# Tokens loaded already turned, with the row factor applied at two evictions and by scaling in place

## The chip, the cores and the metric

One core of one Trainium2 chip runs one launch. Five engines work side by side: TensorE (PE, matmul), VectorE (DVE), ScalarE (ACT), GpSimd (POOL) and SyncE (SP), which issues nearly all transfers. They meet only through semaphores. The metric is the device time of one execution in microseconds (us).

## The reference, cut to what matters

```python
h = x * rsqrt(mean(x*x, -1) + 1e-6) * norm1_w        # x: 512 tokens x 1024
y = h @ w_in                                          # 1024 x 3852, float32
# y is split into the columns of three head groups (forgetting attention,
# retention, gated delta rule) and of their gates:
log_f = log_sigmoid(ff + fox_forget_bias)
log_a = -exp(a_log) * softplus(ga + dt_bias); beta = sigmoid(gb)
qkv = silu(causal_depthwise_conv(concat(gq, gk, gv), conv_w))
x = x + concat(o_fox, o_ret, o_gdn) @ w_out
x = x + hier_moe(rms_norm(x))                         # top-1 group, top-2 of 8 experts
out = rms_norm(x, final_norm_w)
```

The row factor `rsqrt(...)` is one number for each token, `norm1_w` one number for each of the 1024 features. Both can be applied before the product; the row factor can as well be applied to the rows of `y` after it.

## The kernel before, in words

A float32 product is made of three products of reduced operands: each operand is split into a high part (an fp32r copy) and a low part (the operand less its high part), and PE adds high x high, high x low and low x high in one bank of PSUM (`granule`, L750).

**Granules.** The input projection has 15 column groups (`GROUPS`), each of 256 or 260 columns, and each group two granules: the rows of `w_in` in chunks 0 to 3 (even granule) and 4 to 7 (odd). Groups of kind "n" give tokens on partitions (four tiles of tokens, 12 matmuls each and granule, the tokens as the stationary operand), those of kind "t" give columns on partitions (two blocks of 12 matmuls over all 512 tokens). Groups 0 (`zb`, with the gate columns of the delta rule) and 1 (`fv`, with the forget gate) are of kind "n", groups 2 to 7 (`v0` to `q1`) of kind "t".

**The weights' path.** For granule g: SP loads `raw` (L585, three buffers, so from g = 3 on it waits until the low part of g - 3 is made), ACT copies it into `whi` (`weight_high`, L1201, two buffers: it waits until PE has used granule g - 2), POOL subtracts into `wlo` (`weight_low`, L1509), and PE waits for `wlo_done`. POOL does this for every granule; DVE has no part in it.

**The tokens' path.** SP loads four tiles of `x` (L574, tokens on partitions). ACT sums the squares of a tile (`squares`, L1224), DVE takes the reciprocal and multiplies the tile by row factor and by `norm1_w` (`normalize`, L1679), the latter spread over partitions in PSUM by a one-row product (L874). PE turns the tile (`turn_tokens`, L879, eight transposes a tile, those of tiles 2 and 3 between the tiles of granule 0), ACT copies the turned tile into `hHi` (`high_part`, L1229), DVE subtracts into `hLo` (`token_low`, L1693). Granule 0 goes tile by tile behind this.

**What hangs on the first groups.** ACT evicts a group of kind "n" tile by tile (`evac`, L1250). After group 1, DVE computes the gates (`gates`, L1730), a chain of small dependent operations on SBUF with three exponentials of ACT in it, and PE's next task behind granule 5 (`gcum`, L805) waits for its end (`gates_done`). Each engine runs its own list in program order; `AFTER[g]` holds the tasks that follow granule g on every engine. The convolutions of groups 2 to 7 start with four scaled accumulations (ACT L1289, DVE L1723).

The later stages (the triangular solves, attention and retention, the output projection, the routing and the expert loop, whose weights SP loads as buffers come free) are not touched.

Of the kernel before, what the change touches and what calls it, by code (L numbers as in the profile page):

```python
# [23 lines left out]
F32 = mybir.dt.float32  # L24
# [8 lines left out]
P = 128  # L33
# [19 lines left out]
HB = P // 2  # L53

# [31 lines left out]
for _i in range(NIN):  # L86
    AFTER[2 * _i + 1].append(("evac", _i))
AFTER[3].append(("gates",))
# [35 lines left out]
def tensor_orders():  # L124

    a, b = [("par",), ("nb", 0), ("nb", 1)], [("xT", t, i) for t in range(T) for i in range(2)]
    for g in range(GR_IN):
# [3 lines left out]
        for task in AFTER[g]:  # L131
            if task[0] == "vt":
# [126 lines left out]
def build(nc, consts, x, n1w, w_in, foxb, convw, alog, dtb, gnw, w_out, n2w, rgw, rgb, rew, reb,  # L259
# [13 lines left out]
    with ExitStack() as ctx:  # L273
# [31 lines left out]
        PCW = at("PCW", [P, 4, 12], q0 + 288)  # L305
        PGN = at("PGN", [P, P], q0 + 480)
        assert q0 + 480 + 512 <= C0

        hHi = at("hHi", [P, KC, S], R1, F32R)
# [86 lines left out]
        onesr = small[0:1, 640:768]  # L396
# [6 lines left out]
        s_const = sem("s_const"); s_const2 = sem("s_const2"); s_n1 = sem("s_n1"); s_cw = sem("s_cw"); s_par = sem("s_par")  # L403
        s_x = [sem(f"s_x{t}") for t in range(T)]
        raw_full = [sem(f"raw_full{i}") for i in range(3)]
        whi_done = sem("whi_done"); wlo_done = sem("wlo_done"); half_used = sem("half_used")
        ssx_done = sem("ssx_done"); xn_done = sem("xn_done"); hhi_done = sem("hhi_done")
# [121 lines left out]
        rf_done = sem("rf_done"); one_set = sem("one_set"); pass_done = sem("pass_done"); rw_ready = sem("rw_ready"); lg_used = sem("lg_used"); ssp_done = sem("ssp_done"); ssp_sum = sem("ssp_sum"); r2_done = sem("r2_done")  # L529
# [42 lines left out]
        def _(sp):  # L572
            def tokens(t):
                sp.dma_start(X0[:, t, :], x[0, t * P:(t + 1) * P, :]).then_inc(s_x[t], 16)  # L574

            tokens(0)
            tokens(1)
            sp.dma_start(CT[:, 0:NSTAY], consts[:, 0:NSTAY]).then_inc(s_const, 16)

# [10 lines left out]
            for t in range(2, T):  # L590
                tokens(t)
            for g in (1, 2):
                granule(g)
            sp.dma_start(CT[:, NSTAY:], consts[:, NSTAY:]).then_inc(s_const2, 16)
            for dst, src in ((PDT[:, :], dtb[0:1, :].broadcast_to([P, 4])),
# [5 lines left out]
                sp.dma_start(dst, src).then_inc(s_par, 16)  # L601
            def rows_out():
# [15 lines left out]
            for g in range(3, GR_IN + 4):  # L618
# [11 lines left out]
                if 4 <= g < 12:  # L630
                    sp.dma_start(yd.ap().rearrange("(a p) d -> a p d", p=P)[g - 4], zt[:, :]).then_inc(s_zero, 16)
# [105 lines left out]
        def _(pe):  # L737
# [12 lines left out]
            def granule(g, ready=None, between=None, tiles=range(T)):  # L750
                pe.wait_ge(wlo_done, g + 1)
                n, at, parts, chunks, _, w, kind = GRANULES[g]
                hi, lo = high_of(g), low_of(g)
                for b in tiles if kind == "n" else range(2):
# [4 lines left out]
                    if g == 0:  # L759
                        wait_read(pe, ("xT", b, 0))  # L760
                        wait_read(pe, ("xT", b, 1))
                    for c, kc in enumerate(chunks):
                        if kind == "n":
                            tk = slice(b * P, (b + 1) * P)
                            o = ps[:, 0:w]
                            terms = ((hHi[:, kc, tk], hi[:, c, :]), (hHi[:, kc, tk], lo[:, c, :]),
                                     (hLo[:, kc, tk], hi[:, c, :]))
# [32 lines left out]
            def task(k):  # L800
                if k[0] == "vt":
# [3 lines left out]
                elif k[0] == "gcum":  # L805
                    pe.wait_ge(gates_done, 1)
                    ps = begin(k)
# [61 lines left out]
            par = begin(("par",))  # L869
            pe.wait_ge(one_set, 1)  # L870
            pe.wait_ge(s_n1, 16)
            for i in range(2):
                name = ("nb", i)
                end(pe.matmul(begin(name)[:, :], onesr, n1r[:, i * 512:(i + 1) * 512], start=True, stop=True), name)  # L874
            pe.wait_ge(s_const, 16)
            pe.wait_ge(s_cw, 16)
            end(pe.transpose(par[:, 0:48], PW48[:, :], ident[0:48, 0:48]), ("par",))

            def turn_tokens(t):  # L879
                for i in range(2):  # L880
                    pe.wait_ge(xn_done, 2 * t + i + 1)
                    four(("xT", t, i), lambda c, o: pe.transpose(o, X0[:, t, (4 * i + c) * P:(4 * i + c + 1) * P], ident))

            turn_tokens(0)
            turn_tokens(1)
            for g in range(GR_IN):
                granule(g, between=lambda b: turn_tokens(b + 2) if g == 0 and b + 2 < T else None)
                for k in AFTER[g]:
                    task(k)
# [322 lines left out]
        def _(act):  # L1212
# [7 lines left out]
            act.dma_start(n1r[:, :], n1w[0:1, :]).then_inc(s_n1, 16)  # L1220
            act.dma_start(PW48[:, :], convw[0].rearrange("k (b p) -> (k b) p", p=P)).then_inc(s_cw, 16)
            act.wait_ge(one_set, 1)
            act.activation(rs[0:1, 0:1], rs[0:1, 0:1], ACT.Sqrt)
            def squares(t):  # L1224
                act.wait_ge(s_x[t], 16)
                link(act.activation(junk[:, :], X0[:, t, :], ACT.Square, accum_out=ssx[:, t:t + 1]))
                act.activation(ssx[:, t:t + 1], ssx[:, t:t + 1], ACT.Sqrt, scale=1.0 / D, bias=epsm[:, :]).then_inc(ssx_done, 1)

            def high_part(t):  # L1229
# [1008 lines left out]
```

## Time and profile before

| what | us |
|---|---|
| median of 3 runs | 617.63 (617.51 to 618.59) |
| profiled execution, its own time | 617.34 |
| its span | 615.2 |
| PE busy | 581.6 (95%) |
| DVE, ACT, POOL busy | 239.4, 199.4, 187.3 |

The span is the time from the first to the last recorded instruction of the profiled execution, whose own time is 2.1 us longer. In the rows below "busy" of PE contains the modelled ends of pipelined matmuls, so the starts of consecutive matmuls are the better measure of its pace. "L774" is a line of the kernel before. Where a row counts several instructions, its second number runs from the start of the first to the end of the last.

### The profile page before, as it was taken

What the parts mean: (1) busy time and instruction counts of PE and PEld (TensorE: products, weight loads), DVE (VectorE), ACT (ScalarE), POOL (GpSimd) and SP (SyncE); (2) the same over time, 40 slices, a digit from 0 to 9 for tenths busy, and PEclk for the clock granted to TensorE, in tenths of its full rate; (3) what the DMA queues carried; (4) which work ended last, traced back from release to release, by engine and by line L of the source; (5) the groups of instructions that cost most, each with busy time, mean ns of one, the idle gap of its engine ahead of it and who ended that gap; (6) DMA issues with size and microseconds to landing.
All of it is one profiled execution on the core that took longest, in us unless ns stands there. A gap on an engine that the chain in (4) does not pass through costs nothing.

```text
span 615.2 us, 12002 instructions
## 1 busy us (share of the span) xinstructions
PE 581.6 (95%) x4922; PEld 448.5 (73%) x4922; DVE 239.4 (39%) x588; ACT 199.4 (32%) x437; POOL 187.3 (30%) x128
## 2 busy tenths in 40 slices
PE   7999999999999999999999999999999999997794
PEld 5997887799998888866689998666566565654351
DVE  6225454583116712277542146323332232321117
ACT  6444445433323352544635321111111121110113
POOL 1434344173178423432363301111112111120014
PEclk9999999999999999999999999999999999999998
DMA  9656443421221122002698878999999999999976
GB/s 338 206 158 185 139 122 118 137 70 37 70 70 36 36 70 70 1 2 85 280 357 312 313 269 311 366 412 430 425 422 424 425 428 426 421 428 425 419 317 236
DMA packets 44856, 150.62 MB, mean 245 GB/s; under 512 B 8552, under 2 KB 29760, under 8 KB 38274
## 3 DMA queue, kind: packets, MB, share of 16 engines
q1 hardware_dynamic: 40208, 141.67, 60.6%
q0 software_dynamic: 4528, 8.15, 3.6%
q8 instruction: 40, 0.66, 0.4%
q14 instruction: 14, 0.11, 0.1%
q10 hardware_dynamic: 66, 0.03, 0.0%
HBM read 141.69 MB, written 16.27 MB: 257 GB/s over the span
## 4 chain that ended last, share of the span: by engine, by line
PE 62%; DMA 21%; DVE 8%; issue 4%; ACT 2%; POOL 1%; SPq 0%; DVEq 0%; POOLq 0%; ACTq 0%
PE bank L774 30%; DMA xg<-h2d,tok 13%; PE bank L798 9%; DMA w<-in_expert_w_dram 8%; PE bank L1186 5%; PE bank L1140 3%; PE bank L1162 2%; PE bank L1086 1%; DVE Dm L1823 1%; PE bank L1080 1%; PE bank L1100 1%; PE bank L1056 1%; DMA raw<-in_w_in_dram 1%; PE bank L905 1%; PE bank L972 1%
## 5 line engine op out<-in xcount | busy, mean ns | idle before, releaser
L1511 POOL TENSOR_TENSOR wlo<-raw,whi 128x1024 fp32r<-128x1024 f32 (+1 forms) x25 | 59.9, 2398 | 96.7 <-ACT whi L1209 96.7
L774 PE MATMUL bank<-wlo,hHi 128*128 128x256 f32 (+2 forms) x224 | 65.5, 292 | 0.0
L1140 PE MATMUL bank<-w,xT 128*64 128x256 f32 x512 | 59.6, 386 | 5.7 <-issue 5.7
L1633 POOL DMA_INDIRECT yd<-oy,dst x15 | 15.1, 1009 | 162.3 <-DVE oy L2153 162.3
L774 PE MATMUL bank<-whi,hHi 128*128 128x256 f32 (+1 forms) x208 | 60.6, 291 | 2.8 <-DVE cacc L1723 1.4
L1140 PEld LDWEIGHTS bank<-w,xT 128*64 128x64 f32 x512 | 38.3, 140 | 30.9 <-issue 16.1
L1162 PE MATMUL bank<-w,xT 128*64 128x256 f32 x512 | 58.2, 380 | 2.7 <-DMA w<-in_expert_w_dram 2.7
L1186 PE MATMUL bank<-w,hidT 128*64 128x512 f32 x256 | 58.5, 598 | 1.1 <-ACT hidT L1488 1.1
L774 PE MATMUL bank<-whi,hLo 128*128 128x256 f32 (+1 forms) x208 | 59.2, 285 | 0.0
L1162 PEld LDWEIGHTS bank<-w,xT 128*64 128x64 f32 x512 | 36.5, 137 | 21.6 <-DMA w<-in_expert_w_dram 3.6
L2136 DVE SCALAR_TENSOR_TENSOR hid<-bank,slot,sa 128x256 f32<-128x256 f32 x16 | 10.8, 675 | 96.4 <-issue 93.8
L774 PE MATMUL bank<-hHi,wlo 128*128 128x512 f32 x112 | 44.1, 393 | 0.0
L1209 ACT ACTIVATE whi<-raw 128x1024 fp32r<-128x1024 f32 (+1 forms) x25 | 26.6, 1063 | 51.9 <-PE bank L774 50.3
L774 PEld LDWEIGHTS bank<-wlo,hHi 128*128 128x128 f32 x224 | 42.8, 191 | 0.5
L774 PEld LDWEIGHTS bank<-whi,hHi 128*128 128x128 f32 x208 | 39.7, 191 | 4.2 <-DVE cacc L1723 1.8
L1483 ACT ACTIVATE sa<-bank,slot 128x256 f32<-128x256 f32 x16 | 7.6, 474 | 107.8 <-PE bank L1140 101.4
L774 PEld LDWEIGHTS bank<-whi,hLo 128*128 128x128 f32 x208 | 39.7, 191 | 0.0
L1186 PEld LDWEIGHTS bank<-w,hidT 128*64 128x64 f32 x256 | 17.2, 136 | 29.1 <-issue 27.2
L774 PE MATMUL bank<-hHi,whi 128*128 128x512 f32 x96 | 38.2, 398 | 0.0
L774 PE MATMUL bank<-hLo,whi 128*128 128x512 f32 x96 | 37.8, 394 | 0.0
L774 PE MATMUL bank<-whi_tight,hHi 128*128 128x256 f32 (+1 forms) x112 | 36.9, 330 | 0.5 <-issue 0.4
L1723 DVE SCALAR_TENSOR_TENSOR cacc<-bank,PCW,cacc 128x511 f32<-128x511 f32 (+2 forms) x36 | 26.4, 747 | 23.6 <-ACT cacc L1289 22.4
(375 smaller groups left out, 1124.1 us busy)
## 6 DMA issues: line engine op xcount, KB each, us to landing
w<-in_expert_w_dram SPq DMA_DIRECT2D x44, 2048.0 KB, 21.5
raw<-in_w_in_dram SPq DMA_DIRECT2D x24, 512.0 KB, 3.8
w<-in_expert_w_dram SPq DMA_DIRECT2D x8, 1024.0 KB, 7.1
yd<-zt SPq DMA_DIRECT2D x8, 512.0 KB, 5.1
yt<-yd SPq DMA_DIRECT2D x4, 1024.0 KB, 8.6
raw<-in_w_in_dram SPq DMA_DIRECT2D x6, 520.0 KB, 7.2
X<-in_x_dram SPq DMA_DIRECT2D x4, 512.0 KB, 5.8
raw<-in_w_out_dram SPq DMA_DIRECT2D x4, 512.0 KB, 3.4
```

The costliest lines, as they stand in the source:

```text
L774: m = pe.matmul(o, l, r, start=(at == 0 and c == 0 and i == 0), stop=(at == parts - 1 and kc == chunks[-1] and i == 2), skip_group_check=True)
L798: return pe.matmul(o, l, r, start=True, stop=True)
L905: pe.matmul(two[i][:, 0:w], fqT[hp, pr, t * P:(t + 1) * P], fkT[hp, pr, 0:w], start=True, stop=False)
L1140: m = pe.matmul(pb[3][r, 0:FF], xT[:, c, r], w1[u % 4][:, e, c * FF:(c + 1) * FF], start=(c == 0), stop=(c == KC - 1), skip_group_check=True)
L1162: m = pe.matmul(pb[7][r, 0:FF], xT[:, c, r], w3[u % 4][:, e, c * FF:(c + 1) * FF], start=(c == 0), stop=(c == KC - 1), skip_group_check=True)
L1186: m = pe.matmul(pb[5 + n][r, :], hidT[:, c, r], w2[s][:, e, c * D + n * 512:c * D + (n + 1) * 512], start=(c == 0), stop=(c == 1), skip_gr ...
L1209: e.activation(high_of(g), raw_of(g), ACT.Copy).then_inc(whi_done, 1)
L1483: act.activation(sa[:, :], pb[3][:, 0:FF], ACT.Silu, scale=slot[:, u, 0:1]).then_inc(sa_ready, 1)
L1511: pool.tensor_tensor(low_of(g), raw_of(g), high_of(g).bitcast(F32), ALU.subtract).then_inc(wlo_done, 1)
L1633: pool.indirect_dma_start(yd.ap()[:, :], bass.IndirectOffsetOnAxis(ap=dst_i[o][:, 0:1].bitcast(U32), axis=0), oy[o][:, :], None, bounds_ch ...
L1723: j = dve.scalar_tensor_tensor(out=a[:, s:S], in0=psum(name)[:, 0:S - s], scalar=PCW[:, 3 - s, blk:blk + 1], in1=a[:, s:S], op0=ALU.mult, ...
L2136: dve.scalar_tensor_tensor(out=hid[:, :, :].rearrange("q c p -> q p c"), in0=v(pb[7][:, 0:FF]), scalar=slot[:, u, 1:2], in1=v(sa[:, :]), o ...
```

## The change

Two inputs have another layout: `turned` is `x` with features on partitions (128 partitions x 8 chunks x 512 tokens), `lead` holds `norm1_w` and the convolution weights with features on partitions. The kernel still loads `x` as well, for the sums of squares.

- The product with ones, the transposes of `x` and of the convolution weights, `normalize` and `token_low` go. `hHi0` and `hLo0` are made from `turned` times `norm1_w`, without the row factor, chunk by chunk (ACT, then DVE), and serve granules 0 to 3 (groups 0 and 1).
- Granule 0 is run chunk by chunk over four banks (`first_granule`). Its weights' low part is made half by DVE, half by POOL.
- PE runs 30 bf16 products of zeros ahead of it.
- The copies of groups 0 and 1 out of PSUM multiply by the row factor. ACT therefore waits for it ahead of `evac(0)`.
- A task `rb` on PE behind granule 1 spreads the row factor over the partitions. DVE copies it to `RB`, multiplies the eight chunks of `xt0` by it in place, and makes `hLo` of them; ACT makes `hHi` behind granules 1 and 2. Granules 4 and 5 wait for these.
- The constants' first part is loaded behind granule 3, the second part behind granule 4 and the small parameters.

```diff
+AFTER[1].append(("rb",))
         @block.sync
             granule(0)
-            for t in range(2, T):
-                tokens(t)
-            for g in (1, 2):
-                granule(g)
-            sp.dma_start(CT[:, NSTAY:], consts[:, NSTAY:]).then_inc(s_const2, 16)
+            turned_tokens(0)
+            turned_tokens(1)
+            granule(1)
+            turned_tokens(2)
+            turned_tokens(3)
+            tokens(0)
+            tokens(1)
+            granule(2)
+            tokens(2)
+            tokens(3)
+            sp.wait_ge(first_low, 1)
+            granule(3)
+            sp.dma_start(CT[:, 0:NSTAY], consts[:, 0:NSTAY]).then_inc(s_const, 16)
+            granule(4)
...
         @block.tensor
             def granule(g, ready=None, between=None, tiles=range(T)):
                 pe.wait_ge(wlo_done, g + 1)
+                if g in (1, 4, 5):
+                    pe.wait_ge(xlo_done, {1: KC, 4: KC + HK, 5: 2 * KC}[g])
+                H, L = (hHi0, hLo0) if g < 4 else (hHi, hLo)
...
+            def first_granule():
+                n, _, _, chunks, _, w, _ = GRANULES[0]
+                hi, lo = high_of(0), low_of(0)
+                tiles = [begin(("y", n, b)) for b in range(T)]
+                pe.wait_ge(first_low, 1)
+                for c, kc in enumerate(chunks):
+                    pe.wait_ge(xlo_done, kc + 1)
+                    if c == HK // 2:
+                        pe.wait_ge(wlo_done, 1)
+                    for b in range(T):
...
+                if k[0] == "rb":
+                    pe.wait_ge(s_const, 16)
+                    pe.wait_ge(ssx_done, 2)
+                    four(k, lambda t, o: mm(o, rx[:, t:t + 1].broadcast_to([P, P]), ident))
...
+            zb = zt.bitcast(BF16)
+            pe.wait_ge(zero_set, 1)
+            for _ in range(WARM):
+                pe.matmul(pb[7][:, 0:256], zb[:, 0:P], zb[:, 0:256], start=True, stop=True)
         @block.scalar
+            def high_part(c):
+                act.wait_ge(s_xt[c // 2], 16)
+                act.activation(hHi0[:, c, :], xt0[:, c, :], ACT.Copy, scale=n1p[:, c:c + 1]).then_inc(hhi_done, 1)
+
+            def scaled_high(c):
+                act.wait_ge(tok_scaled, c + 1)
+                act.activation(hHi[:, c, :], xt0[:, c, :], ACT.Copy, scale=n1p[:, c:c + 1]).then_inc(hhi_done, 1)
+
+            weight_high(act, 0)
+            act.wait_ge(s_lead, 16)
+            for c in range(HK):
+                high_part(c)
+            weight_high(act, 1)
+            for c in range(HK, KC):
+                high_part(c)
             squares(0)
             squares(1)
+            weight_high(act, 2)
             squares(2)
             squares(3)
+            act.activation(ssx, ssx, ACT.Sqrt, scale=1.0 / D, bias=epsm[:, :]).then_inc(ssx_done, 1)
+            act.wait_ge(ssx_done, 2)
...
-                        cp = lambda dst, src: act.activation(dst, src, ACT.Copy)
+                        cp = lambda dst, src: act.activation(dst, src, ACT.Copy, scale=rx[:, t:t + 1] if n < 2 else 1.0)
...
+                if g in (1, 2):
+                    for c in range((g - 1) * HK, g * HK):
+                        scaled_high(c)
         @block.vector
+            dve.wait_ge(whi_done, 1)
+            hc = slice(0, HK // 2)
+            dve.tensor_tensor(low_of(0)[:, hc, :], raw_of(0)[:, hc, :], high_of(0)[:, hc, :].bitcast(F32),
+                              ALU.subtract).then_inc(first_low, 1)
+            for c in range(KC):
+                dve.wait_ge(hhi_done, c + 1)
+                dve.scalar_tensor_tensor(out=hLo0[:, c, :], in0=xt0[:, c, :], scalar=n1p[:, c:c + 1],
+                                         in1=hHi0[:, c, :].bitcast(F32), op0=ALU.mult, op1=ALU.subtract).then_inc(xlo_done, 1)
+            dve.wait_ge(ssx_done, 1)
+            dve.reciprocal(rx, ssx).then_inc(ssx_done, 1)
+            name = ("rb",)
+            wait_full(dve, name)
+            release(dve.tensor_copy(RB[:, :], psum(name)[:, :]), name)
+            wait_read(dve, name)
+            dve.wait_ge(xlo_done, KC)
+            for c in range(KC):
+                dve.tensor_tensor(xt0[:, c, :], xt0[:, c, :], RB[:, :], ALU.mult).then_inc(tok_scaled, 1)
+            for c in range(KC):
+                dve.wait_ge(hhi_done, KC + c + 1)
+                dve.scalar_tensor_tensor(out=hLo[:, c, :], in0=xt0[:, c, :], scalar=n1p[:, c:c + 1],
+                                         in1=hHi[:, c, :].bitcast(F32), op0=ALU.mult, op1=ALU.subtract).then_inc(xlo_done, 1)
```

## Rows read from the trace of the kernel before

**Rows 1.** The page, part 1: busy time, share of the span and instructions of each engine.

```profile
PE 581.6 (95%) x4922; PEld 448.5 (73%) x4922; DVE 239.4 (39%) x588; ACT 199.4 (32%) x437; POOL 187.3 (30%) x128
```

**Rows 2.** Chain of waits, 0 to 130 us: start, us, what ran (count).

```profile
20.04 19.05 PE bank L774 x156
50.17 0.04 issue
50.21 0.62 PE bank L798 x4
52.04 11.29 PE bank L774 x48
```

**Rows 3.** Timeline, opening: start, us, engine, line, operation, shapes, count, [idle before, releaser].

```profile
4.53 1.06 ACT L1226 ACTIVATE junk<-X 128x1024 f32<-128x1024 f32 x1 [1.35 <-DMA X<-in_x_dram]
8.26 1.07 ACT L1209 ACTIVATE whi<-raw 128x1040 fp32r<-128x1040 f32 x1 [0.77 <-DMA raw<-in_w_in_dram]
11.87 0.59 PE L774 MATMUL bank<-whi,hHi 128*128 128x260 f32 x1 [1.15 <-POOL wlo L1511]
```

**Rows 4.** Table by window: PE, PEld, DVE, ACT, POOL busy, granted clock, DMA share, GB/s.

```profile
0.00:5.00 5.00, 2.64 (x3) 1.16 (x4) 1.64 (x6) 1.95 (x3) 0.20 (x4) 1.00 0.63 214
5.00:10.00 5.00, 4.41 (x17) 3.14 (x16) 3.19 (x7) 4.17 (x10) 0.59 (x1) 1.00 1.03 387
10.00:15.00 5.00, 3.85 (x18) 3.45 (x17) 4.37 (x9) 3.94 (x9) 1.81 (x1) 1.00 1.09 399
```

**Rows 5.** DVE groups, 0 to 150 us: count, busy us, mean ns, idle before.

```profile
L1686 DVE SCALAR_TENSOR_TENSOR X<-X,keep,bank 128x512 f32<-128x512 f32 x8 | 5.6, 744 | 0.1
L1699 DVE TENSOR_TENSOR hLo<-bank,hHi 128x512 fp32r<-128x512 f32 x8 | 5.1, 684 | 2.0 <-ACT hHi L1233 2.0
```

**Rows 6.** ACT groups, 0 to 150 us.

```profile
L1233 ACT ACTIVATE hHi<-bank 128x512 fp32r<-128x512 f32 x8 | 4.3, 589 | 1.9 <-PE bank L882 1.9
L1209 ACT ACTIVATE whi<-raw 128x1040 fp32r<-128x1040 f32 x4 | 4.3, 1074 | 3.7 <-PE bank L774 2.8 <-DMA raw<-in_w_in_dram 0.8 <-ACT small L1257 0.2
L1226 ACT ACTIVATE junk<-X 128x1024 f32<-128x1024 f32 x4 | 4.2, 1056 | 1.4 <-DMA X<-in_x_dram 1.4
L1257 ACT ACTIVATE fv<-bank 128x256 f32<-128x256 f32 x4 | 1.5, 385 | 3.3 <-PE bank L774 3.3
```

**Rows 7.** Timeline of POOL, 40 to 52 us.

```profile
40.87 2.40 POOL L1511 TENSOR_TENSOR wlo<-raw,whi 128x1024 fp32r<-128x1024 f32 x1 [3.95 <-ACT whi L1209]
45.85 2.40 POOL L1511 TENSOR_TENSOR wlo<-raw,whi 128x1024 fp32r<-128x1024 f32 x1 [2.59 <-ACT whi L1209]
51.71 2.40 POOL L1511 TENSOR_TENSOR wlo<-raw,whi 128x1024 fp32r<-128x1024 f32 x1 [3.45 <-ACT whi L1209]
```

**Rows 8.** Timeline of DVE and ACT, 39 to 51 us: the gates.

```profile
39.63 0.17 DVE L1736 TENSOR_TENSOR small<-small,PDT 128x16 f32<-128x16 f32 x1 [19.74 <-ACTq L1273]
42.10 0.23 ACT L1313 ACTIVATE small<-small 128x32 f32<-128x32 f32 x1
42.56 0.74 DVE L1742 TENSOR_SCALAR small<-small 128x32 f32<-128x32 f32 x1 [2.23 <-ACT small L1315]
45.98 2.33 DVE L1749 SCALAR_TENSOR_TENSOR small<-small 128x32 f32<-128x32 f32 x1
```

**Rows 9.** Timeline of DVE, then of POOL, 307 to 312 us.

```profile
307.34 2.63 DVE L1878 TENSOR_TENSOR mix<-mix,keep 128x1024 f32<-128x1024 f32 x2
...
308.13 0.75 POOL L1602 TENSOR_TENSOR hLo<-foxF,hHi 128x128 fp32r<-128x128 f32 x1 [1.05 <-ACT foxF L1428]
308.85 3.38 POOL L1607 TENSOR_TENSOR mix<-mix,oret 128x1024 f32<-128x1024 f32 x1
```

**Rows 10.** Table by window, 583 to 585 us, columns as in rows 4.

```profile
583.00:585.00 2.00, 2.00 (x12) 1.28 (x10) 0.00 (x0) 0.00 (x0) 0.47 (x1) 0.50 1.10 451
```

**Rows 11.** Timeline of PE, 582 to 593 us.

```profile
582.62 5.05 PE L1140 MATMUL bank<-w,xT 128*64 128x256 f32 x32 [2.63 <-issue]
...
588.82 3.67 PE L1162 MATMUL bank<-w,xT 128*64 128x256 f32 x32
```

More of the change, by code:

```diff
@@ L53 @@
 HB = P // 2
+WARM = 30
 FQ, FK, FV, FFG = 0, 256, 512, 768
@@ L124, in tensor_orders @@
 def tensor_orders():
-    a, b = [("par",), ("nb", 0), ("nb", 1)], [("xT", t, i) for t in range(T) for i in range(2)]
+    a, b = [], []
     for g in range(GR_IN):
@@ L573, in tokens, with turned_tokens @@
             def tokens(t):
[L574 to L578, printed above, removed]
+                sp.dma_start(X0[:, t, :], x[0, t * P:(t + 1) * P, :]).then_inc(s_x[t // 2], 16)
+            def turned_tokens(i):
+                sp.dma_start(xt0[:, 2 * i:2 * i + 2, :].rearrange("p c n -> p (c n)"),
+                             turned[:, 2 * i * S:(2 * i + 2) * S]).then_inc(s_xt[i], 16)
             def granule(g):
@@ L617, in _ @@
             sp.wait_ge(zero_set, 1)
-            for g in range(3, GR_IN + 4):
+            for g in range(5, GR_IN + 4):
                 granule(g)
@@ L781, in granule @@
                         between(b)
+            def first_granule():
[8 more added lines that the diff above has]
+                    for b in range(T):
+                        tk = slice(b * P, (b + 1) * P)
+                        for i, (l, r) in enumerate(((hHi0[:, kc, tk], hi[:, c, :]), (hHi0[:, kc, tk], lo[:, c, :]),
+                                                    (hLo0[:, kc, tk], hi[:, c, :]))):
+                            m = pe.matmul(tiles[b][:, 0:w], l, r, start=(c == 0 and i == 0), stop=False, skip_group_check=True)
+                m.then_inc(half_used, 1)
             def four(name, f):
@@ L867, in task @@
                         four(("u0", t), lambda h, o: mm(o, Um[i][:, h, :], vb[:, t, h, :]))
[L869 to L885, printed above, removed]
+            zb = zt.bitcast(BF16)
+            pe.wait_ge(zero_set, 1)
+            for _ in range(WARM):
+                pe.matmul(pb[7][:, 0:256], zb[:, 0:P], zb[:, 0:256], start=True, stop=True)
             for g in range(GR_IN):
-                granule(g, between=lambda b: turn_tokens(b + 2) if g == 0 and b + 2 < T else None)
+                if g:
+                    granule(g)
+                else:
+                    first_granule()
                 for k in AFTER[g]:
@@ L1365, in _ @@
                 behind = [k for k in AFTER[g] if k[0] == "xt" or k == ("fin", 0)]
-                if not plain and not behind and (g % 2 or g < 2 or GROUPS[g // 2 - 1][1] not in CONVN):
+                if g and not plain and not behind and (g % 2 or GROUPS[g // 2 - 1][1] not in CONVN):
                     weight_high(act, g + 2)
@@ L1678, in _ @@
                 dve.sem_inc(one_ahead, 1)
-            def normalize(t):
-                dve.wait_ge(ssx_done, t + 1)
-                link(dve.reciprocal(rx[:, t:t + 1], ssx[:, t:t + 1]))
-                for i in range(2):
-                    cs = slice(i * 512, (i + 1) * 512)
-                    if t == 0:
-                        wait_full(dve, ("nb", i))
-                    dve.scalar_tensor_tensor(out=X0[:, t, cs], in0=X0[:, t, cs], scalar=rx[:, t:t + 1], in1=psum(("nb", i))[:, :],
-                                             op0=ALU.mult, op1=ALU.mult).then_inc(xn_done, 1)
-                if t == T - 1:
-                    dve.wait_ge(xn_done, 2 * T)
-                    for i in range(2):
-                        dve.sem_inc(free[BANK[("nb", i)][0]], 1)
```

93 lines of the change are left out of this document (33 added, 60 removed).

## The prediction, made before the changed kernel was run

> **What bounds the kernel now.** The page comes first: PE is busy 95% of the span [rows 1]. So what matters is when PE's unbroken work starts and where it later stops. The chain of waits says both. From 20.04 to 39.1 us it is 156 matmuls in a row, 0.122 us each, which makes 5.8 us for a granule of kind "n"; two granules of kind "t" take 11.1 us by their starts, the run of 48 at L774 ending with 11.29 [rows 2]. In the opening the timeline shows what PE waits for: the first tile of x is there at 4.5, the first weights at 8.3, POOL's low part lets granule 0 start at 11.87 [rows 3]. Working back from 39.1, granule 2 starts at about 27.4. The second place is 50.2 us: granule 5 has just ended (about 50.0), and the gates' last operation on DVE releases `gcum` at 50.17, so PE and the gates arrive together. A gain in the opening is worth something only if the gates come earlier too. Behind that PE is hardly ever stopped, and the loads of the expert weights hang on buffers that the earlier stages free, so I take a shift at 52 us to reach the end whole.
>
> **The opening, part by part.** A transfer lands some 1.2 us after the running sum of bytes reaches it: the first tile of x (0.52 MB) starts ACT at 4.53; the first weights, fourth in the queue with 1.87 MB up to them, start it at 8.26, and the rates put 1.87 MB at 7.1 [rows 3, 4]. The new order by the same rates (1.07 MB by 5 us, 3.0 by 10, then 0.39 to 0.4 a us): weights 0 at 4.5, turned 0 at 6.2, turned 1 at 7.5, weights 1 at 8.9, turned 3 at 11.6, x tile 1 at 14.2, x tile 3 (5.8 MB in all, 2.1 MB more than the same list before) at 18.2, first constants at about 20.3.
>
> ACT's copy of the weights (1.07) ends at 5.6 [rows 6]. DVE and POOL then each take half of the low part. DVE's new operations read two operands from SBUF, and the trace shows what that means beside POOL. L1749 is one of a series of small operations and lasts 2.33 us; it ends at 48.31, when POOL's subtraction of 45.85 to 48.25 is over; L1742, started at 42.56, ends at 43.30 behind the one of 40.87 to 43.27 [rows 7, 8]. The other way round, POOL's L1602 (0.75) and L1607 (3.38) are stretched while two multiplications of DVE run back to back, and L1602 gets in between those two [rows 9]. So they take turns: POOL waits for at most one operation of DVE, and DVE for the whole 2.40 us of POOL. Operations with one operand in PSUM (L1686, L1699) don't show it, and all of DVE's token work before was of that kind [rows 5]. The Trainium skill, "SBUF — State Buffer", section Who interferes with whom, states it for a DVE instruction with two SBUF inputs against a GpSimd one that reads SBUF: the second to issue waits for all of the first. The trace agrees (2.33 us); a sum without this rule is the rival "no turns" below.
>
> The halves (0.6 and 1.2) are thus over at 7.5; `hLo0` costs some 0.70 a chunk (744 ns at L1686, less the overlap of neighbours: 5.6 us for 8), so granule 0 starts at 8.3, 3.6 us earlier than now, runs 5.8 us and ends at 14.1. The 30 products of zeros lie ahead of 8.3 and cost nothing (if PE were still at half pace for some of granule 0, the next wait would hide up to 1.5 us of it). POOL's second low part takes its turn at 10.3 to 12.7, in the middle of `hLo0`; the last four chunks follow until 15.5, so granule 1 runs 15.6 to 21.4. The row factor: x tile 3 at 18.2, two sums of squares at 1.25 (1056 plus the accumulator's read), root and reciprocal, 21.2 [rows 6]. It and the constants come just before PE asks. `rb` is eight passes of 128 columns, unseen in this form: from the 0.62 of four small ones [rows 2], 0.5 to 1.2, I take 0.9. Granule 2 starts at 22.3 instead of 27.4: 5.1 us are won here. If the loads came 1 us late, the row factor would be late by 0.8 and so would granule 2.
>
> **Behind it, the price.** DVE copies RB (0.7, from PSUM), scales eight chunks (8 x 0.64, from 5.1 us for 8 at L1699) and makes eight low parts (8 x 0.70) [rows 5]: 11.4 us of which none was there before (the token work ended at 19.9 and DVE then rested until 39.63 [rows 8]). Into them fall POOL's low parts for granules 3, 4 and 5. ACT can copy the weights of granule 3 only after `evac(0)` (four tiles, 0.55 each [rows 6]), POOL asks at 24; those of granule 4 after granule 2 has been used, POOL asks at 30; both block DVE 2.4 us. The first four low parts are done at 22.4 + 0.7 + 5.1 + 4.8 + 2.8 = 35.8, with the hand-overs 35.9. PE ends granule 3 at 22.3 + 11.6 = 33.9 and waits 2.0 us for them. Call this point H = 35.9, the start of granule 4.
>
> From H: `scaled_high` of chunk 7, `evac(1)` and the copy for granule 5 put POOL's third turn at H + 0.7 to H + 1.1, behind those four chunks, so the last four low parts end at H + 2.8 + 2.4 = H + 5.2. Only then does DVE start the gates: 0.7 to the point where ACT is asked (four small operations), 0.7 for the exponentials and hand-overs (42.10 to 42.56, and two hand-overs, the table being loaded already; between 0.5 and the 2.2 of the row), and the chain. The chain took 42.56 to 50.17 = 7.6, of which 0.55 + 2.15 were turns of POOL: 4.9 without [rows 8, 2]. POOL's turn for granule 6 falls into it for certain, since ACT's copy stands right behind the exponentials: 2.4. End at H + 5.2 + 0.7 + 0.7 + 4.9 + 2.4 = H + 13.9. But PE has used granule 5 at H + 11.1, ACT copies granule 7's weights until H + 12.8 (before, it lagged the end of granule 5 in the same way and POOL began at 51.71, behind the gates [rows 7]), and POOL takes one more turn in the last microsecond of the chain: H + 12.8 + 2.4 + about 1.0 = H + 16.2 = 52.1. `gcum` starts at 52.1 against 50.21: 1.9 us later, the 5.1 won and 7.0 lost.
>
> PE now idles from 47.0 to 52.1. Before, an idle 2.63 us at 580 is followed by a granted clock of 0.50 in 583 to 585 us, the lower level (1.2 GHz), and by 32 matmuls in 5.05 instead of 3.67 us [rows 10, 11]. I take that price, 1.4 us; its bounds are 0 (the clock stays at 2.4 GHz) and twice that, 2.8, as the low stretch may last longer. The later constants land near 27 us, and `gcum`'s new wait for them costs nothing; the zeros' stores and the parameters move by one granule, beside PE's work, and nothing asks for them before 100 us. The copies with a scale are taken as long as those without.
>
> Sum: 617.34 + 1.9 + 1.4 = 620.6 for an execution like the profiled one, whose time is 0.3 below the median of the runs: 620.9.
>
> **Rivals.** *The last turn misses the gates.* If the chain is 1 us shorter against H, or granule 5 ends 1 us later, POOL's turn for granule 7 comes after it and `gcum` starts at H + 13.9 = 49.8, 0.4 earlier than now; with 0 to 1.4 us for the clock 617.2 to 618.6. For it: the margin is 1.0 us in a sum of a dozen terms, and a slower clock behind the wait at H would delay granule 5 by just that. Against: every term has a row.
> *No turns, or cheap ones.* The low parts end near 33.9 without POOL's turns, granule 4 starts at once, the gates at 34.5, and PE is 5.1 us ahead at `gcum`: 612.5. One or two turns less heavy, as when POOL slips in between without holding DVE for its whole length, give 613 to 616. For it: rows 9 show DVE's second multiplication hardly delayed by the small L1602. Against: 2.33 us for L1749.
> *More DMA.* The added 2.1 MB or the later constants come 1 to 2 us late, granule 2 with them: 622 to 623, from the point where the row factor is later than 21.4. Against it: the rates held 0.39 to 0.40 MB/us.
> That the change doesn't do what it says I rule out only in part: the row factor may be so late that the first two groups gain nothing; that is the same case.
>
> **How the numbers follow.** The forecast 0.45 (half of it with 0 to 1 us for the clock, 619.5 to 620.5), the missed turn 0.17, no or cheap turns 0.28, more DMA 0.10. A measurement of this kernel tells 0.2%, 1.24 us, from no change. Faster than 616.4: the cheap turns and the edge of the missed one, 0.30. Within: 0.17, the rest of the missed turn and some cheap one. Slower than 618.9: 0.53. The range 612.5 to 622.5 leaves out the worst DMA and double clock cases and a gain beyond 5.1; the forecast's own range is 619.3 to 622.3.
>
> **What would show it.** Right: DVE's scaling and low parts with single operations of 2.5 to 3 us that end with POOL's; PE waiting some 2 us ahead of granule 4 and some 5 ahead of `gcum`, with a granted clock under 1 behind it; granule 0 near 8.3, granule 2 near 22.3. Wrong: even 0.7 us operations on DVE beside a busy POOL, the gates beginning before 38 us, or `gcum` before 50. If PE leaves `gcum` later than now and the end is not later, the shift was absorbed further on, and the first paragraph fails.

## The result, and the profile after

The changed kernel took 621.85 us (median of 7 runs, 618.41 to 622.42) where the kernel before took 617.51 (616.54 to 618.59) beside it: ratio 1.0062, interval 1.0045 to 1.0079. Twelve further runs on another occasion gave 618.86 (616.41 to 622.38), ratio 1.0020, 0.9999 to 1.0042. So it is slower in the first set, not clearly so in the second, and within a set it scatters over 4.0 and 6.0 us where the kernel before scatters over 2.1 and 2.6. The profiled execution took 621.19, its span is 618.8 us against 615.2: 3.6 us more. The page, part 1:

```profile
PE 578.8 (94%) x4923; PEld 446.1 (72%) x4923; DVE 255.1 (41%) x594; ACT 205.3 (33%) x441; POOL 187.7 (30%) x128
```

PE has slightly less to do than in [rows 1], DVE 16 us more. The opening went as forecast. From the timeline of the changed kernel, PE, DVE and POOL (start, us, engine, line, operation, shapes, count, [idle before, releaser]):

```profile
2.00 6.22 PE L908 MATMUL bank<-zt 128*128 128x256 bf16 x30 [2.00 <-DVE zt L1703]
8.65 0.36 PE L811 MATMUL bank<-whi,hHi 128*128 128x260 f32 x1 [0.42 <-DVE hLo L1716]
15.55 0.36 PE L789 MATMUL bank<-whi,hHi 128*128 128x260 f32 x1 [0.91 <-DVE hLo L1716]
21.93 1.16 PE L829 MATMUL bank<-CT,keep 128*128 128x128 f32 x8 [0.35 <-DMA CT<-const_dram]
35.91 0.47 PE L789 MATMUL bank<-hHi,whi 128*128 128x512 f32 x1 [1.27 <-issue]
50.94 0.62 PE L829 MATMUL bank<-small,CT 128*128 128x16 f32 x4 [3.65 <-DVE small L1782]
```

The six rows are the zeros, the starts of granule 0 (11.87 in [rows 3]), granule 1, `rb`, granule 4 and `gcum` (50.21 in [rows 2]). Granule 2's first matmul starts at 22.85 us against some 27.4 before, so PE is 4.5 us ahead behind `rb`; at `gcum` it is 0.7 late. DVE and POOL in between:

```profile
23.85 7.14 DVE L1726 TENSOR_TENSOR xt<-xt,RB 128x512 f32<-128x512 f32 x8
30.92 9.69 DVE L1729 SCALAR_TENSOR_TENSOR hLo<-xt,lead_in,hHi 128x512 fp32r<-128x512 f32 x8
40.53 0.16 DVE L1756 TENSOR_TENSOR small<-small,PDT 128x16 f32<-128x16 f32 x1
...
41.71 0.18 DVE L1762 TENSOR_SCALAR small<-small 128x32 f32<-128x32 f32 x1 [0.49 <-ACT small L1341]
...
42.97 3.64 DVE L1768 SCALAR_TENSOR_TENSOR small<-small 128x32 f32<-128x32 f32 x7
...
48.33 0.16 DVE L1781 TENSOR_TENSOR small<-small 128x4 f32<-128x4 f32 x1
48.53 2.36 DVE L1782 TENSOR_TENSOR small<-small 128x4 f32<-128x4 f32 x1
```

```profile
24.89 2.55 POOL L1540 TENSOR_TENSOR wlo<-raw,whi 128x1040 fp32r<-128x1040 f32 x1 [4.53 <-ACT whi L1235]
30.38 2.89 POOL L1540 TENSOR_TENSOR wlo<-raw,whi 128x1024 fp32r<-128x1024 f32 x1 [2.94 <-ACT whi L1235]
36.62 2.77 POOL L1540 TENSOR_TENSOR wlo<-raw,whi 128x1024 fp32r<-128x1024 f32 x1 [3.35 <-ACT whi L1235]
42.99 2.45 POOL L1540 TENSOR_TENSOR wlo<-raw,whi 128x1024 fp32r<-128x1024 f32 x1 [3.59 <-ACT whi L1235]
48.52 2.35 POOL L1540 TENSOR_TENSOR wlo<-raw,whi 128x1024 fp32r<-128x1024 f32 x1 [3.09 <-ACT whi L1235]
```

Lay POOL's five low parts over DVE's rows. One falls into the scalings, two into the token low parts, one into the chain's seven operations at L1768 (3.64 us for what takes 1.55 in short_lows, without the turn), and the last begins 0.01 us before the gates' very last operation, on 128x4 numbers, which takes 2.36 us instead of 0.16. POOL's own three rows of 2.55 to 2.89 are longer than its 2.44 us at 17.9, where DVE rests, by less than one DVE operation of 0.6 to 0.7 us: POOL waits for the one in progress. Behind `gcum`, the table by window (PE, PEld, DVE, ACT, POOL busy, granted clock, DMA share, GB/s) and the chain of waits:

```profile
50.00:52.00 2.00, 1.06 (x9) 1.03 (x10) 1.96 (x3) 0.90 (x1) 0.87 (x1) 1.00 0.18 67
52.00:54.00 2.00, 2.00 (x9) 1.30 (x9) 1.93 (x4) 0.63 (x1) 0.00 (x0) 0.52 0.84 170
54.00:56.00 2.00, 2.00 (x8) 1.54 (x7) 1.88 (x6) 0.00 (x0) 0.00 (x0) 0.62 0.91 351
```

```profile
53.28 12.40 PE bank L789 x48
```

The granted clock fell to the lower level (0.52 in 52 to 54 us) after the pause of 3.65 us. From `gcum` to granule 6 it is 53.28 - 50.94 = 2.34 us instead of 1.83, and granules 6 and 7 take 12.40 instead of 11.29 [rows 2]: 1.6 us. With the 0.7 at `gcum` the lag is 2.3 us, and it stays 2.3 to the start of the expert loop: that loop's first run of 32 matmuls, in the chain of the changed kernel and then of the kernel before:

```profile
384.26 3.60 PE bank L1166 x32
```

```profile
381.94 3.60 PE bank L1140 x32
```

The last 1.3 of the 3.6 us arise in the expert loop and behind it. Over that stretch, from the loop's first matmul to the end of the span, the ten other traces below differ from the kernel before by -0.1 to 0.9 us, so 1.3 is the largest of eleven; what it comes from is not shown.

### The profile page after: what moved, and what is told of

Read it like the earlier page. It is cut to its first block, busy times and chain, and to the rows that moved or that the text cites. A ratio compares the mean times of both kernels' runs of the same rounds, so it can differ in the third digit from the quotient of the medians.

```text
span 618.8 us, 12012 instructions
## 1 busy us (share of the span) xinstructions
PE 578.8 (94%) x4923; PEld 446.1 (72%) x4923; DVE 255.1 (41%) x594; ACT 205.3 (33%) x441; POOL 187.7 (30%) x128
## 4 chain that ended last, share of the span: by engine, by line
PE 64%; DMA 19%; DVE 11%; issue 3%; ACT 1%; POOL 1%; SPq 0%; DVEq 0%; POOLq 0%; ACTq 0%
PE bank L789 26%; PE bank L829 9%; DMA w<-in_expert_w_dram 8%; PE bank L1212 6%; DMA xg<-h2d,tok 5%; PE bank L1188 5%; PE bank L1166 4%; DMA CT<-const_dram 2%; PE bank L1112 2%; PE bank L1126 2%; DMA yd<-oy,dst 2%; DVE hLo L1729 1%; DMA yt<-yd 1%; DVE Dm L1843 1%; PE bank L1106 1%
## 5 line engine op out<-in xcount | busy, mean ns | idle before, releaser
L1540 POOL TENSOR_TENSOR wlo<-raw,whi 128x1024 fp32r<-128x1024 f32 (+1 forms) x24 | 58.6, 2442 | 92.9 <-ACT whi L1235 92.9
L1166 PE MATMUL bank<-w,xT 128*64 128x256 f32 x512 | 58.2, 380 | 4.9 <-issue 4.9
L1188 PE MATMUL bank<-w,xT 128*64 128x256 f32 x512 | 58.2, 380 | 3.2 <-DMA w<-in_expert_w_dram 3.2
L789 PE MATMUL bank<-wlo,hHi 128*128 128x256 f32 (+2 forms) x208 | 60.4, 290 | 0.0
L789 PE MATMUL bank<-whi,hHi 128*128 128x256 f32 (+1 forms) x192 | 55.3, 288 | 2.3 <-DVE cacc L1743 1.4
L789 PE MATMUL bank<-whi,hLo 128*128 128x256 f32 (+1 forms) x192 | 54.1, 282 | 0.0
L789 PEld LDWEIGHTS bank<-wlo,hHi 128*128 128x128 f32 x208 | 39.2, 188 | 0.5
L789 PEld LDWEIGHTS bank<-whi,hHi 128*128 128x128 f32 x192 | 36.2, 188 | 3.3 <-DVE cacc L1743 1.8
L789 PEld LDWEIGHTS bank<-whi,hLo 128*128 128x128 f32 x192 | 36.1, 188 | 0.0
L1743 DVE SCALAR_TENSOR_TENSOR cacc<-bank,lead_in,cacc 128x511 f32<-128x511 f32 (+2 forms) x36 | 26.4, 747 | 21.4 <-ACT cacc L1315 20.4
```

The lines of the kernel that those rows point to most:

```text
L789: m = pe.matmul(o, l, r, start=(at == 0 and c == 0 and i == 0), stop=(at == parts - 1 and kc == chunks[-1] and i == 2), skip_group_check=True)
L1166: m = pe.matmul(pb[3][r, 0:FF], xT[:, c, r], w1[u % 4][:, e, c * FF:(c + 1) * FF], start=(c == 0), stop=(c == KC - 1), skip_group_check=True)
L1188: m = pe.matmul(pb[7][r, 0:FF], xT[:, c, r], w3[u % 4][:, e, c * FF:(c + 1) * FF], start=(c == 0), stop=(c == KC - 1), skip_group_check=True)
L1540: pool.tensor_tensor(low_of(g), raw_of(g), high_of(g).bitcast(F32), ALU.subtract).then_inc(wlo_done, 1)
L1743: j = dve.scalar_tensor_tensor(out=a[:, s:S], in0=psum(name)[:, 0:S - s], scalar=PCW[:, 3 - s, blk:blk + 1], in1=a[:, s:S], op0=ALU.mult, ...
```

## The experiments

Each ran beside the kernel before; all were also profiled. They fall into three occasions, on which the kernel before had medians of 617.98 (again to short_lows), 617.80 (dve_lows to no_zeros) and 617.34 (the last two), so across occasions the ratios are the better measure. Medians in us, with the ratio to before and its interval:

| kernel | median (range), runs | ratio (interval) | span profiled |
|---|---|---|---|
| again | 618.86 (616.41 to 622.38), 12 | 1.0020 (0.9999 to 1.0042) | 615.7 |
| last_turn | 618.07 (615.91 to 619.04), 12 | 0.9999 (0.9988 to 1.0010) | 613.7 |
| fill | 617.86 (617.19 to 619.46), 12 | 0.9997 (0.9986 to 1.0007) | 615.6 |
| short_lows | 613.95 (612.83 to 614.60), 6 | 0.9930 (0.9914 to 0.9947) | 611.1 |
| dve_lows | 613.73 (612.60 to 615.03), 6 | 0.9934 (0.9919 to 0.9948) | 610.7 |
| late_gates | 621.49 (620.55 to 622.10), 6 | 1.0058 (1.0045 to 1.0070) | 619.1 |
| turn_fill | 616.76 (615.61 to 617.64), 12 | 0.9984 (0.9976 to 0.9993) | 613.8 |
| no_zeros | 621.10 (618.48 to 622.42), 12 | 1.0044 (1.0029 to 1.0060) | 618.5 |
| const_first | 613.25 (612.69 to 613.94), 6 | 0.9936 (0.9922 to 0.9950) | 610.9 |
| dve_lows_again | 613.61 (612.97 to 614.34), 6 | 0.9940 (0.9926 to 0.9954) | 611.5 |

### again: the changed kernel once more

No edit.

> The changed kernel once more, for a second trace of it. Turns theory (POOL's low parts stop DVE, the gates end late, PE pauses ahead of gcum and its clock falls): gcum starts at 50.9 as in the first trace, within 0.3, the first matmul of granule 8 stands 2.3 us later than before, and the end is 2.3 to 3.6 us later; the 1.3 us by which the first trace grew beyond granule 8's lag are not in every execution. Rival (the last 1.3 us belong to the change, by its 2.1 MB more of transfers): again 3.6 us and the same stretch behind the expert loop.

The timeline of DVE, POOL and PE at the end of the gates, the table by window, and the chain of waits:

```profile
48.42 0.16 DVE L1782 TENSOR_TENSOR small<-small 128x4 f32<-128x4 f32 x1
...
48.43 2.38 POOL L1540 TENSOR_TENSOR wlo<-raw,whi 128x1024 fp32r<-128x1024 f32 x1 [3.11 <-ACT whi L1235]
...
48.64 0.62 PE L829 MATMUL bank<-small,CT 128*128 128x16 f32 x4 [1.44 <-DVE small L1782]
```

```profile
50.00:52.00 2.00, 2.00 (x9) 1.47 (x7) 1.93 (x4) 1.44 (x2) 0.81 (x1) 0.66 0.18 40
52.00:54.00 2.00, 2.00 (x6) 1.56 (x5) 1.97 (x6) 0.00 (x0) 0.00 (x0) 0.50 0.84 169
```

```profile
50.46 12.88 PE bank L789 x48
```

My expectation for `gcum` missed: 48.6, not 50.9. In this execution DVE's last operation began 0.01 us before POOL's turn and got through. The clock fell all the same after 1.44 us of pause, and granules 6 and 7 took 12.88 us instead of 11.29: `gcum` was 1.6 us earlier than before, the matmuls at 121.7 us stand where they stood, and the span is 615.7. So one kernel has two outcomes at the gates, a few hundredths of a microsecond apart, and the extra 1.3 us of the first trace's end are not in this one (0.5).

### last_turn: POOL's low part of granule 7 behind the gates

```diff
             for g in range(GR_IN):
...
+                if g + 2 == 7:
+                    pool.wait_ge(gates_done, 1)
                 if ("decx", 0) not in AFTER[g]:
                     weight_low(g + 2)
```

> The changed kernel, but POOL makes the low part of granule 7's weights only when the gates are done. Turns theory: the gates' last operation takes 0.2 instead of 2.4 us, gcum starts at 48.8 instead of 50.9, PE's pause ahead of it is 1.6 instead of 3.7 us and its clock stays up: 2.1 + 1.6 = 3.7 us less than the changed kernel, about 0.9 to 1.4 us less than before. Rival (the gates are late for another reason and POOL's subtraction is only beside them): gcum at 50.7 or later and no change of time.

```profile
48.52 0.16 DVE L1784 TENSOR_TENSOR small<-small 128x4 f32<-128x4 f32 x1
...
48.76 2.36 POOL L1540 TENSOR_TENSOR wlo<-raw,whi 128x1024 fp32r<-128x1024 f32 x1 [3.35 <-DVE small L1784]
...
48.74 0.62 PE L829 MATMUL bank<-small,CT 128*128 128x16 f32 x4 [1.45 <-DVE small L1784]
```

The trace has what was expected: the last operation 0.16 us, `gcum` at 48.74, the clock at 1.00 throughout (windows 48 to 58 us), a span 1.5 us under that of before. The median does not, and with it the expected gain of 0.9 to 1.4 us is missed: 618.07, that of before. The profiled execution was the fastest of the twelve (615.91). The record has a mean granted clock for every execution: 0.992 to 0.995 in the four at or below 617.06 us, 0.989 to 0.992 in the eight slower ones. That fits a fall of the clock in most of them, but only the one execution has a trace that says where; turn_fill tests it. The slow end of the changed kernel's scatter is gone (619.04 against 622.4).

### fill: zeros on PE while it waits for the gates

```diff
                 elif k[0] == "gcum":
+                    for _ in range(32):
+                        pe.matmul(pb[7][:, 0:256], zb[:, 0:P], zb[:, 0:256], start=True, stop=True)
                     pe.wait_ge(gates_done, 1)
```

> The changed kernel, with 32 products of zeros (bf16, 128x256) on PE between granule 5 and its wait for the gates. Clock theory: gcum starts at 50.9 as in the changed kernel, but gcum and granule 6 run at full pace, and the whole is 1.6 us less than the changed kernel. Rival (the slow start of granule 6 comes from its operands or from the pause's refill, not from the clock): no change of time, granted clock in 52 to 56 us still near 0.55.

```profile
47.30 3.67 PE L844 MATMUL bank<-zt 128*128 128x256 bf16 x32
50.81 0.52 PE L831 MATMUL bank<-small,CT 128*128 128x16 f32 x4
```

```profile
52.00:54.00 2.00, 2.00 (x12) 1.50 (x11) 1.93 (x6) 0.20 (x1) 0.00 (x0) 1.00 0.85 139
```

With PE busy through the pause the clock stays at 1.00 and granules 6 and 7 take 11.30 us: the slow start is the clock. `gcum` starts at 50.81 here because of the zeros themselves (in this execution the gates' last operation took 0.16 us and ended at 48.85), so the kernel shows the late start without the fall: a lag of 0.6 us at `gcum`, and a scatter of 2.3 us instead of 6. The median of 617.86 is 1.0 us under that of again beside it, where 1.6 was expected.

### short_lows: POOL's turns made short

```diff
             def weight_low(g):
                 pool.wait_ge(whi_done, g + 1)
-                pool.tensor_tensor(low_of(g), raw_of(g), high_of(g).bitcast(F32), ALU.subtract).then_inc(wlo_done, 1)
+                w = slice(0, 8) if 3 <= g <= 7 else slice(0, None)
+                pool.tensor_tensor(low_of(g)[:, :, w], raw_of(g)[:, :, w], high_of(g)[:, :, w].bitcast(F32),
+                                   ALU.subtract).then_inc(wlo_done, 1)
```

> The changed kernel, but POOL's subtraction for granules 3 to 7 covers 8 columns of each chunk only; the rest of these low parts is left as it was (part of the computation is left out). Turns theory: the eight scalings take 5.1 instead of 7.1 us, the eight low parts 5.6 instead of 9.7, the gates end at about 41 to 42, PE does not wait ahead of granule 4 or gcum and starts gcum near 45.8: 5.1 us ahead of now by gcum, 4.4 us less than before (613), 6 to 8 less than the changed kernel. Rival (DVE's operations on two SBUF operands are slow by themselves): the two groups still take some 7 and 9.7 us and the time is that of the changed kernel.

```profile
24.08 4.97 DVE L1728 TENSOR_TENSOR xt<-xt,RB 128x512 f32<-128x512 f32 x8
28.97 5.38 DVE L1731 SCALAR_TENSOR_TENSOR hLo<-xt,lead_in,hHi 128x512 fp32r<-128x512 f32 x8
...
25.59 0.49 POOL L1541 TENSOR_TENSOR wlo<-raw,whi 128x32 fp32r<-128x32 f32 x1 [4.52 <-ACT whi L1235]
```

The same sixteen operations of DVE take 4.97 and 5.38 us instead of 7.14 and 9.69, `gcum` starts at 45.78 without a pause, and the time is 613.95, 4.0 below before. The gates' last operation ends at 43.43, later than the 41 to 42 expected, which costs nothing, as PE asks at 45.78. DVE's operations on two SBUF operands are not slow by themselves; the 6.5 us between the two kernels' rows are three turns of POOL, 2.2 each.

### dve_lows: the low parts of granules 3 to 5 on DVE

```diff
+            def low_on_dve(g):
+                dve.wait_ge(wlo_done, g)
+                dve.wait_ge(whi_done, g + 1)
+                dve.tensor_tensor(low_of(g), raw_of(g), high_of(g).bitcast(F32), ALU.subtract).then_inc(wlo_done, 1)
...
             for c in range(KC):
                 dve.tensor_tensor(xt0[:, c, :], xt0[:, c, :], RB[:, :], ALU.mult).then_inc(tok_scaled, 1)
+                if c == 0:
+                    low_on_dve(3)
+            low_on_dve(4)
             for c in range(KC):
...
+            low_on_dve(5)
...
             for g in range(GR_IN):
+                if g + 2 == 6:
+                    pool.wait_ge(gates_done, 1)
-                if ("decx", 0) not in AFTER[g]:
+                if ("decx", 0) not in AFTER[g] and g + 2 not in (3, 4, 5):
                     weight_low(g + 2)
```

> The changed kernel, with the low parts of granules 3, 4 and 5 made by DVE itself (1.25 us each, in the places of its list where their high parts are ready) and POOL making that of granule 6 only when the gates are done. Turns theory: four turns of 2.1 us become three operations of 1.25, so the last low part of the tokens is ready near 38, the gates near 44.5, PE does not wait ahead of granule 4 or gcum and starts gcum at 45.8: the run of short_lows with a correct sum, 613.5 to 614. Rival (what short_lows gained came from less work of POOL as such, not from DVE's freedom): 616 or more.

```profile
24.68 1.24 DVE L1724 TENSOR_TENSOR wlo<-raw,whi 128x1040 fp32r<-128x1040 f32 x1
25.84 4.30 DVE L1734 TENSOR_TENSOR xt<-xt,RB 128x512 f32<-128x512 f32 x7
...
31.36 5.38 DVE L1740 SCALAR_TENSOR_TENSOR hLo<-xt,lead_in,hHi 128x512 fp32r<-128x512 f32 x8
...
43.83 0.16 DVE L1794 TENSOR_TENSOR small<-small 128x4 f32<-128x4 f32 x1
```

All work is done and the time is that of short_lows: 613.73, 4.1 below before and 5 to 8 below the changed kernel. DVE makes a low part in 1.24 us, little more than half of the 2.2 us that POOL's takes from it. POOL here still does all its other work, so what short_lows gained was DVE's freedom. The gates end at 43.99 instead of 50.17 [rows 2], before granule 5 does. This version beats both kernels; dve_lows_again repeats it (613.61).

### late_gates: 0.45 us more in the chain

```diff
                 link(dve.tensor_tensor(lfc[:, 8:12], lfc[:, 4:8], lf[:, 4:8], ALU.add))
+                for _ in range(2):
+                    link(dve.tensor_copy(lfc[:, 4:8], lf[:, 0:4]))
```

> The changed kernel, with two more small copies on DVE in the gates' chain, 0.45 us in all. In the first trace POOL's turn for granule 7 caught the gates' last operation, in the second it began in the same tenth of a microsecond and missed it. Race theory: with 0.45 us more the chain is always caught, gcum starts at 50.9 to 51.3 with a pause of 3.7 to 4.1 us and a slow granule 6 in every execution, so all times lie between 620 and 623 and the low ones near 616.5 to 618 are gone. Rival (the wide spread of the changed kernel comes from elsewhere, from the transfers of the expert loop for instance): the spread of 6 us stays, with a median 0.5 us up.

```profile
48.66 2.41 DVE L1783 COPY small<-small 128x4 f32<-128x4 f32 x2
...
48.46 2.38 POOL L1540 TENSOR_TENSOR wlo<-raw,whi 128x1024 fp32r<-128x1024 f32 x1 [3.13 <-ACT whi L1235]
...
51.32 1.03 PE L829 MATMUL bank<-small,CT 128*128 128x16 f32 x4 [4.09 <-DVE small L1784]
```

Chain of waits:

```profile
54.60 12.04 PE bank L789 x48
```

All six times lie between 620.55 and 622.10: the low half of the changed kernel's scatter is gone. On the same occasion no_zeros, whose chain is not lengthened, has five of twelve executions at or under 619.20. With last_turn, which takes the slow half away, that shows the two halves of the scatter as the turn that catches or misses the chain. The clock cost more here than in the first trace: it fell within the pause (0.84 in 48 to 50 us, 0.50 behind), from `gcum` to granule 6 it is 3.28 us instead of 1.83, and granules 6 and 7 take 12.04 instead of 11.29: 2.2 us.

### turn_fill: last_turn with 12 zeros in the pause

The edit of last_turn, and that of fill with `range(12)`.

> The kernel last_turn (POOL's low part of granule 7 behind the gates), with 12 products of zeros on PE in the pause ahead of gcum. In last_turn's trace gcum was 1.5 us earlier than before and the span 1.5 us shorter, but its median time was that of before. Clock theory: in most of its executions the clock fell after the pause of 1.4 us and gave back the 1.5 us; with the zeros it can't, and the median is 1.3 to 1.5 us below before, about 616.5. Rival (the 1.5 us are lost further on, in the expert loop): the median stays near 618.

Timeline of PE:

```profile
47.12 1.49 PE L844 MATMUL bank<-zt 128*128 128x256 bf16 x12
48.71 0.62 PE L831 MATMUL bank<-small,CT 128*128 128x16 f32 x4
```

The median is 616.76, below before (ratio 0.9984, 0.9976 to 0.9993), with `gcum` at its place, and the clock at 1.00 from 46 to 58 us. Each against the kernel before beside it, last_turn is 0.1 us above and this kernel 1.0 below: 1.1 us between them, from two occasions, with intervals that overlap a little (0.9988 to 1.0010 and 0.9976 to 0.9993). In last_turn the slower executions had the lower mean clock; here there is no such order. So the likely reading is that the clock gave back most of what last_turn had won at `gcum` in most of its executions, after the same pause of 1.45 us that left it alone in the profiled one. No trace of such an execution is there to show it.

### no_zeros: without the zeros at the start

`WARM = 0` instead of 30.

> The changed kernel without the 30 products of zeros at the start. The prediction's step: PE runs granule 0 at half pace for about 3 us, which makes it end 1.5 us later, at 15.9 instead of 14.5; the wait for the tokens' low parts at 15.5 hides 0.9 of it, and the row factor and the constants at 21.9 hide the rest, so rb starts at most 0.2 us later and the time is the changed kernel's. Rival (the zeros matter): granules 0 and 1 run cold to the end and rb starts at 24 or later, and the time is 2 us above the changed kernel's.

Chain of waits, then timeline, then the table by window:

```profile
8.43 7.60 PE bank L811 x48
16.04 5.78 PE bank L789 x48
...
53.83 12.50 PE bank L789 x48
```

```profile
21.65 1.05 PE L829 MATMUL bank<-CT,keep 128*128 128x128 f32 x8
```

```profile
10.00:12.00 2.00, 2.00 (x11) 2.00 (x10) 1.30 (x2) 1.79 (x4) 1.91 (x1) 1.00 1.02 406
```

Granule 0 takes 7.60 us instead of some 5.8, and `rb` starts no later than with the zeros (21.65 against 21.93). The median of 621.10 lies between those of the two occasions of the changed kernel, inside its scatter, so times alone settle nothing here. The trace settles the opening: the zeros don't bring `rb` forward. It doesn't settle whether they bear on what comes later. In this trace the turn caught the chain and the clock's fall cost 2.7 us (3.28 instead of 1.83 from `gcum` at 50.55 to granule 6, 12.50 instead of 11.29 behind), the most of all traces.

### const_first, dve_lows_again: the constants ahead of granule 3

const_first against dve_lows:

```diff
-            sp.wait_ge(first_low, 1)
-            granule(3)
             sp.dma_start(CT[:, 0:NSTAY], consts[:, 0:NSTAY]).then_inc(s_const, 16)
+            sp.wait_ge(first_low, 1)
+            granule(3)
```

> The kernel dve_lows, with the first part of the constants loaded ahead of granule 3's weights instead of behind them. In dve_lows PE idles 0.57 us ahead of rb until the constants land at 22.0, while the row factor is there at 21.1 and granule 1 has ended at 21.4. Theory (rb is held by the constants): they land 1.3 us sooner, rb starts at 21.4 to 21.6 and everything behind is 0.4 to 0.6 us earlier: some 0.5 us less than dve_lows, 613.2. Rival (DVE's list, not PE's, sets the time up to gcum, or a granule 3 that lands later takes it back): no change against dve_lows.

> The kernel dve_lows once more, beside const_first on the same chip: 613.5 to 614, gcum started at 45.6 to 45.9 with no pause ahead of it and the granted clock at 1.00 through 58 us.

PE's row of `rb` in const_first and in dve_lows_again:

```profile
21.67 1.06 PE L829 MATMUL bank<-CT,keep 128*128 128x128 f32 x8
```

```profile
22.14 1.16 PE L829 MATMUL bank<-CT,keep 128*128 128x128 f32 x8 [0.40 <-DMA CT<-const_dram]
```

DVE's low part of granule 3 in the same two:

```profile
25.05 1.24 DVE L1724 TENSOR_TENSOR wlo<-raw,whi 128x1040 fp32r<-128x1040 f32 x1 [0.85 <-ACT whi L1235]
```

```profile
24.96 1.24 DVE L1724 TENSOR_TENSOR wlo<-raw,whi 128x1040 fp32r<-128x1040 f32 x1 [0.20 <-ACT whi L1235]
```

The wait for the constants is gone and `rb` starts 0.5 us earlier. But little of it lasts: DVE, ahead by the same amount, now waits 0.85 us for ACT's copy of granule 3's weights, its low part starts 0.1 us later than in dve_lows_again, and at `gcum` PE is 0.2 us ahead (45.62 against 45.79). The rival, that DVE's list sets the time up to `gcum`, is right for the rest. The medians, 613.25 and 613.61, differ by 0.4, but their ranges overlap over most of their length with six runs each, so a gain is not shown.

## Why the prediction was right

**The opening.** Forecast: granule 0 at 8.3, granule 1 at 15.6, the row factor at 21.2, `rb` at 21.4, granule 4 at 35.9. Measured: 8.65, 15.55, 21.34, 21.93, 35.91. `rb` came 0.5 late because the constants landed at 21.9, 1.6 later than the rates gave. That granule 4 is right to the hundredth is luck: DVE began its copy of `RB` 0.7 late (23.13 for 22.4), and the scaling, four low parts and two turns took some 0.7 less than the 12.7 summed for them, the turns costing 2.2 us each and not 2.4. The halves of the first low part, and POOL's turn in the middle of `hLo0`, are there. The zeros cost nothing ahead of `rb`, as said, and bring nothing there; no_zeros shows it.

**The turns.** The central step, that POOL's low parts stop DVE's new operations for their whole length and DVE stops POOL for one operation, is shown by short_lows. Five turns were forecast behind `rb` and five came, each in its place. The signs named came too, smaller: a single operation of 2.90 us, PE waiting 1.3 us ahead of granule 4 (not 2) and 3.7 ahead of `gcum` (not 5).

**The last turn.** Forecast: it takes the last microsecond of the chain, `gcum` at H + 16.2 = 52.1. Measured: it takes only the last operation, and in the second trace misses it. So the step that was off is this one. The mis-sized term is the distance between the chain's end and POOL's turn, 1.0 forecast and 0.0 to 0.2 measured: the last four token low parts ended at H + 4.7 and not H + 5.2, the exponentials with their hand-overs took 0.5 and not 0.7, and the turn inside the chain cost 2.1 and not 2.4. So `gcum` started 0.7 later than before, not 1.9, where it was caught, and 1.6 earlier where not. The rival "the last turn misses the gates" and my forecast are two executions of one kernel, and `gcum` before 50 us, which again has, was one of my own signs of being wrong. I had given them chances of one kernel each and did not see that a margin of this size makes a kernel that does both; late_gates and last_turn hold it on either side.

**The clock.** 1.4 us forecast from [rows 10, 11], with bounds of 0 and 2.8. Measured: 1.6 in both traces of the changed kernel (0.5 in `gcum` and 1.1 behind it in the first, all behind it in the second), 2.2 in late_gates, 2.7 in no_zeros, 0 in last_turn. So the bounds held, and the single number is at the low end of what a fall costs here. That it would fall after a pause of 1.4 us too I had left open; in again it did.

**The sum.** 620.9 forecast, 621.85 and 618.86 measured. In the first trace 0.7 + 1.6 = 2.3 us are traced to the steps; the other 1.3 came in the expert loop or behind it, where again grew by 0.5 and last_turn by 0.0. That part is not explained; the forecast's 620.9 is close in part because this stands in for the 1.2 us by which the last turn was over-sized. Luck is in the direction too: of the nineteen executions nine lie in the forecast's own range of 619.3 to 622.3, eight under 618.9 and two above 622.3, and the two sets of runs drew these outcomes in different shares, so that one median is clearly slower than before and the other is not.

**What the change does without the turns.** The rival "no turns" said 612.5; short_lows and dve_lows have 613.95 and 613.73. The idea of the change was worth 4 us, and giving the turned tokens to DVE operations that POOL's subtractions stop cost all of it.

## What to carry to other kernels

When work moves from PSUM operands to two SBUF operands on DVE, count POOL's instructions that run beside it, at their full length each; a subtraction that takes POOL 2.4 us can be cheaper on DVE itself at 1.24. When two engines meet at a place by a margin of a tenth of a microsecond, expect two times, not one, and look at the list of runs before the median. And when PE is made to wait, even for 1.4 us, add the clock: a fall cost 1.6 to 2.7 us in the traces here, and turn_fill, with twelve products of zeros in the pause, was 1.1 us better against its own kernel before than last_turn without them.

## What the runs showed of the hardware that I had not expected

- The same pause of PE, 1.44 and 1.45 us, was followed by a granted clock of 0.50 to 0.66 in one execution (again) and of 1.00 in another (last_turn). With PE kept busy it stayed at 1.00 (fill, turn_fill).
- One operation on 128x4 numbers of DVE took 0.16 us when it began 0.01 us before POOL's subtraction and 2.36 us when it began 0.01 us behind it.
- A copy out of PSUM by ACT with the factor taken from SBUF takes 0.46 us for 256 columns (L1283 of the changed kernel) against 0.385 [rows 6]; I had taken them as equal, which cost nothing here.
- The granted clock of the table by window does not show the slow start of PE's first matmuls. In no_zeros they start 0.22 us apart from 8.43 to 12.03 us and 0.12 apart from there on, with 1.00 in the table all the while; in the opening the spacing of the starts says more than the clock's column.
- The same fall of the clock has no fixed price: 1.6 us (the changed kernel, twice), 2.2 (late_gates), 2.7 (no_zeros).
